# Expert 0's rows: seven tiles gathered ahead, the last added by one-hot products; W1[0] split during the output projection; the last one-hots on GpSimd

## What is computed

```python
x = x + concat([yc, ya]) @ w_out
xn = rms_norm(x, norm_ffn_w)                    # the rows that the experts read
g = argmax(xn @ w_group + b_group)              # 1 of 4 groups
top2 of (xn @ w_expert + b_expert)[group g]     # 2 of its 8 experts
h = silu(xb @ w1[e]) * (xb @ w3[e])             # for each of 32 experts, on its tokens xb
x = x + gate * (h @ w2[e])
```

## Time and profile before

| | us |
|---|---|
| median of three runs | 1163.4 (1162.27 to 1164.91) |
| the profiled execution, its own time | 1164.24 |
| its span in the trace | 1162.1 |
| PE busy | 1096.3 (94%) |
| DVE busy | 900.1 (77%) |
| ACT busy | 718.6 (62%) |
| mixer | 0 to about 419 |
| output projection and routing | about 419 to 550 |
| experts | about 550 to 1122 |
| scatter, read back, combine, store | 1122 to 1162 |

### The profile page before, as it was taken

The page is one execution under the profiler, slowest core; times in us unless marked ns, Lnnn a source line. Parts: engine busy times, 40 slices in busy tenths (PEclk is TensorE's granted clock), DMA queues, the critical chain, the costliest instruction groups (busy, mean ns, idle before and its releaser), DMA issues. The chain is left out here.

```text
span 1162.1 us, 16798 instructions
## 1 busy us (share of the span) xinstructions
PE 1096.3 (94%) x5766; PEld 894.9 (77%) x5766; DVE 900.1 (77%) x1033; ACT 718.6 (62%) x882; POOL 139.7 (12%) x192
## 2 busy tenths in 40 slices
PE   8999999999999899997999999999999999999950
PEld 7887777778777668885878888888888888888840
DVE  5505957678575772567989999999999999999947
ACT  5423555646643571112878888888888888888830
POOL 1001000010000120001021110111111111101000
PEclk9999999999999999997999999999999999999985
DMA  7111231313213253003999999999999999999529
GB/s 232 46 35 39 90 89 59 107 39 107 67 46 95 103 214 142 37 37 133 425 427 422 396 384 396 386 384 396 382 383 390 382 392 383 390 387 387 214 77 375
DMA packets 77117, 275.29 MB, mean 237 GB/s; under 512 B 20752, under 2 KB 51600, under 8 KB 63888
## 3 DMA queue, kind: packets, MB, share of 16 engines
q1 hardware_dynamic: 66272, 253.69, 57.6%
q0 software_dynamic: 9216, 16.80, 3.8%
q10 hardware_dynamic: 1584, 4.20, 0.9%
HBM read 259.57 MB, written 31.85 MB: 251 GB/s over the span
## 5 line engine op out<-in xcount | busy, mean ns | idle before, releaser
L1198 DVE TENSOR_TENSOR e_lo<-W,e_hi 128x1024 fp32r<-128x1024 f32 x384 | 451.9, 1219 | 24.5 <-ACT e_hi L1192 21.7
L1192 ACT ACTIVATE e_hi<-W 128x1024 fp32r<-128x1024 f32 x384 | 403.4, 1060 | 94.7 <-PE ps L1163 88.7
L1161 PE MATMUL ps<-e_hi,xT_hi 128*128 128x512 f32 x496 | 196.3, 396 | 1.9 <-DVE xT_lo L1920 1.0
L1163 PE MATMUL ps<-e_lo,xT_hi 128*128 128x512 f32 x496 | 193.7, 390 | 0.0
L1162 PE MATMUL ps<-e_hi,xT_lo 128*128 128x512 f32 x496 | 193.1, 389 | 0.0
L472 PE MATMUL ps<-xnT_hi,w_hi 128*128 128x512 f32 x320 | 129.0, 403 | 1.6 <-DVE u L861 0.6
L472 PE MATMUL ps<-xnT_hi,w_lo 128*128 128x512 f32 x320 | 128.0, 400 | 0.0
L472 PE MATMUL ps<-xnT_lo,w_hi 128*128 128x512 f32 x320 | 125.3, 392 | 0.0
L900 DVE TENSOR_TENSOR_SCAN kept<-kept,start_at 128x1024 f32<-128x1024 f32 (+7 forms) x64 | 88.9, 1389 | 29.1 <-ACT kept L702 29.1
L1161 PEld LDWEIGHTS ps<-e_hi,xT_hi 128*128 128x128 f32 x496 | 93.5, 189 | 20.9 <-DVE xT_lo L1920 1.2
L1163 PEld LDWEIGHTS ps<-e_lo,xT_hi 128*128 128x128 f32 x496 | 93.1, 188 | 19.9
(11 more groups left out here) (244 smaller groups left out, 1706.9 us busy)
## 6 DMA issues: line engine op xcount, KB each, us to landing
W<-in_w_dram SPq DMA_DIRECT2D x96, 2048.0 KB, 15.2
w_raw<-in_w_in_dram SPq DMA_DIRECT2D x20, 512.0 KB, 4.1
yy<-y_rows SPq DMA_DIRECT2D x7, 1024.0 KB, 12.7
xt<-in_x_dram SPq DMA_DIRECT2D x8, 512.0 KB, 3.7
w_out_raw<-in_w_out_dram SPq DMA_DIRECT2D x8, 512.0 KB, 6.4
xn_rows<-xn SPq DMA_DIRECT2D x8, 512.0 KB, 2.6
out_dram<-x ACTq DMA_DIRECT2D x7, 512.0 KB, 9.1
x<-in_x_dram SPq DMA_DIRECT2D x2, 1536.0 KB, 10.7
```

The costliest lines, as they stand in the source:

```text
L1161: pe.matmul(o, xs_hi[:, k], e_hi[:, p, cols], start=(k == 0), stop=False)
L1163: mm = pe.matmul(o, xs_hi[:, k], e_lo[:, p, cols], start=False, stop=(k == last))
L1192: act.activation(e_hi[:, p], flat[:, p * D:(p + 1) * D], ACT.Copy).then_inc(s["hi_made"], 1)
L1198: dve.tensor_tensor(e_lo[:, p], flat[:, p * D:(p + 1) * D], e_hi[:, p], ALU.subtract).then_inc(s["lo_made"], 1)
```

## The change

- DVE makes, in `rank`, a code of each token of expert 0 (its rank plus one, or zero), and from it one one-hot matrix for each tile (`first_one_hots`). PE's `first_list` multiplies seven of them by token numbers, DVE writes `first_token`, and GpSimd gathers expert 0's rows of tiles 0 to 6 while tile 7 is still being routed. `first_rows_gathered` multiplies them by the identity into the banks of `xT`, in accumulation; `first_rows_last` adds tile 7's rows, which are still in SBUF in `xn2[1]`, by its one-hot. `first_turn_x` goes.
- The order on PE: `first_rows_gathered` and two products of the table stand ahead of the count of tile 7; the table's last two products stand between the two halves of gate 0. The 34 transposes that nobody reads go.
- ACT and DVE split W1[0] in tiles 5 and 6 of the projection, into buffers of its own (`e0_hi`, `e0_lo`); W3[0] then needs no free piece.
- The last four pairs of one-hots are made by GpSimd, after the first gather. `xg[1]` is gathered when the whole table is made.
- PE in round 0: gate 0, two pieces of up 0, turn of the overflow list, two pieces of up 0, turn of `xg[1]`. DVE in round 0: pieces 0, 1 of W3[0], `pick_blocks`, piece 2, `list_blocks`, piece 3, gates, piece 0 of W1[1], `x1T_lo`, piece 1.
- SP: W3[0] and W1[1] when `xg[0]` has landed, W3[1] when `xg[1]` has landed, W2[0] after the list is turned, W1[2] after gate 0.

```diff
@@ SP
                 for m in range(NT):
-                    if m == NT - 1:
-                        sp.wait_ge(mixed, 2 * NT)
-                        sp.dma_start(W3[0], w3_v[0]).then_inc(expert_w[0][1], 16)
...
+                sp.wait_ge(mixed, 2 * NT)
                 sp.wait_ge(s_e["gathered"][0], 16)
+                sp.dma_start(W3[0], w3_v[0]).then_inc(expert_w[0][1], 16)
                 sp.dma_start(W1[1], w1_v[1]).then_inc(expert_w[1][0], 16)
+                sp.wait_ge(s_e["gathered"][1], 16)
                 sp.dma_start(W3[1], w3_v[1]).then_inc(expert_w[1][1], 16)
...
+                sp.wait_ge(s_e["freed"], used(gate_start(0) + PIECES))
                 load(W1, w1_v, 2, 0, 0, gate_start(0))
@@ GpSimd
-                for b in range(2):
-                    pool.wait_ge(xn2_stored[b], 16 * (NT // 2))
+                pool.wait_ge(xn2_stored[0], 16 * (NT // 2))
+                pool.wait_ge(xn2_stored[1], 16 * (NT // 2 - 1))
+                pool.wait_ge(first_listed, 1)
+                gather_rows(pool, xg[0], first_token, s_e["gathered"][0], S - P)
+                for n in range(HOTS - 4, HOTS):
+                    k, m = n % 2, n // 2
+                    pool.wait_ge(placed, 3 + m - (NT - 2))
+                    pool.wait_ge(table_step, n - NOH + 1)
+                    pool.tensor_scalar(of_slot[n % NOH], iota[:, 0:P], slot[:, k, m:m + 1], None, ALU.is_equal).then_inc(hot_late, 1)
+                    pool.tensor_scalar(of_column[n % NOH], iota_column, column[:, k, m:m + 1], pair_code[k][:, m:m + 1],
+                                       ALU.is_equal, ALU.mult).then_inc(hot_late, 1)
+                pool.wait_ge(xn2_stored[1], 16 * (NT // 2))
                 pool.wait_ge(routed, 1)
-                for e in range(2):
-                    gather_rows(pool, xg[e], slot_token[:, e:e + 1], s_e["gathered"][e])
+                gather_rows(pool, xg[1], slot_token[:, 1:2], s_e["gathered"][1])
@@ PE
                     if m == 7:
+                        count_before(2)
                         route(7, 0)
-                        count_before(2)
...
+                def first_list():
+                    bank, c0 = FIRST_AT
+                    pe.wait_ge(first_hots, NT - 1)
+                    for m in range(NT - 1):
+                        mm = pe.matmul(ps[:, bank, c0:c0 + 1], first_hot[:, m], token_less[:, m:m + 1], start=(m == 0), stop=(m == NT - 2))
+                    mm.then_inc(first_summed, 1)
+
+                def first_rows_gathered():
+                    pe.wait_ge(s_e["gathered"][0], 16)
+                    pe.wait_ge(x2_made, 2 * NT)
+                    for k in range(KT):
+                        pe.matmul(psf[:, k * P:(k + 1) * P], xg[0][:, k:D:KT], ident, start=(k % 4 == 0), stop=False)
+
+                def first_rows_last():
+                    pe.wait_ge(first_hots, NT)
+                    pe.wait_ge(xn2_made, NT + 1)
+                    for h in range(2):
+                        for k in range(4 * h, 4 * h + 4):
+                            mm = pe.matmul(psf[:, k * P:(k + 1) * P], xn2[1][:, k:D:KT], first_last, start=False, stop=(k % 4 == 3))
+                        mm.then_inc(s_e["turned"] if h else half_turned, 1)
...
+                first_list()
                 turn(NT - 1, 1)
                 route(NT - 1, 1)
+                first_rows_gathered()
+                table(12, 14)
                 count_before(3)
                 count_all()
-                table(12, 16)
-                for i in range(20):
-                    pe.transpose(ps[:, 4, 0:P], ident, ident)
...
+                first_rows_last()
...
                 def first_gate():
...
+                    pe_product(pe, s_e, 0, xT_hi, xT_lo, [ps[:, 2]], 2, KT - 1, (0, 1), **own)
+                    table(14, 16)
                     pe.wait_ge(s_e["xT_made"], 1)
...
+                        pe_product(pe, s_e, up_start(0), xT_hi, xT_lo, [ps[:, 3]], 2, KT - 1, (0, 1))
+                        overflow_list()
+                        pe_product(pe, s_e, up_start(0), xT_hi, xT_lo, [ps[:, 3]], 2, KT - 1, (2, 3))
+                        pe_turn_x(pe, s_e, 1, 1, 1)
+                        return
@@ ACT
+                        if m == 5:
...
+                            act_split(act, s_e, gate_start(0), W1[0], hi=e0_hi, free=True)
...
+                    act_split(act, s_e, up_start(e), W3[b], free=isinstance(e, int) and e == 0)
                     if isinstance(e, int) and e == 0:
+                        act.wait_ge(s_e["freed"], used(gate_start(0) + PIECES))
                         act_xT(act, s_e, 1)
@@ DVE
+                    link(dve.scalar_tensor_tensor(first_code[:, ms], earlier[:, :, 0], 1.0, chosen[:, ms, 0], ALU.add, ALU.mult))
+                    if i == 3:
+                        first_one_hots(NT - 1, NT)
...
+                        dve.wait_ge(first_summed, 1)
+                        dve.tensor_scalar(first_token, ps[:, FIRST_AT[0], FIRST_AT[1]:FIRST_AT[1] + 1], 4.0 * S, None, ALU.add).then_inc(first_listed, 1)
...
                     if isinstance(e, int) and e == 0:
-                        dve_split(dve, s_e, gate_start(0), W1[0], (2, 3))
+                        dve_split(dve, s_e, up_start(0), W3[0], (0, 1))
+                        pick_blocks()
+                        dve_split(dve, s_e, up_start(0), W3[0], (2,))
+                        list_blocks()
+                        dve_split(dve, s_e, up_start(0), W3[0], (3,))
                         make_gates()
...
+                        dve_split(dve, s_e, gate_start(1), W1[1], (0,))
                         dve_xT(dve, s_e, 1)
-                        dve_split(dve, s_e, gate_start(1), W1[1], (0, 1))
+                        dve_split(dve, s_e, gate_start(1), W1[1], (1,))
                         dve_hid(dve, s_e, 0, up_start(0))
...
+                ask_gates()
                 flag_blocks()
+                dve.wait_ge(table_step, HOTS)
+                slots(slice(0, NE))
```

More of the change, by code:

```diff
@@ L1151, in pe_turn_x, with pe_product @@
             mm.then_inc(s["turned"], 1)
-        def pe_product(pe, s, start, xs_hi, xs_lo, out, per_piece, last, pieces=range(PIECES)):
+        def pe_product(pe, s, start, xs_hi, xs_lo, out, per_piece, last, pieces=range(PIECES), hi=e_hi, lo=e_lo):
             for p in pieces:
@@ L1624, in round_of @@
                 def round_of(e, b, rounds, y_rounds=None, last=False):
[L1625 removed]
+                    if not (isinstance(e, int) and e <= 1):
                         act.wait_ge(expert_w[b][0], 16 * rounds)
```

140 lines of the change are left out of this document (81 added, 59 removed).

## The result

| | before | after |
|---|---|---|
| median, six runs each | 1163.53 us (1162.27 to 1165.78) | 1169.12 us (1168.17 to 1169.71) |
| the profiled execution, its own time | 1164.24 | 1169.59 |
| its span | 1162.1 | 1167.9 |
| last matmul of the output projection, start | 529.78 | 531.21 |
| gate 1, start | 563.26 | 567.58 |

The ratio of the medians is 1.0044, 95% interval 1.0031 to 1.0057: the changed kernel is 3.6 to 6.6 us slower. The forecast was 1164.1 with a range to 1167.8, so the prediction was wrong, on the slow side. By the trace the step that failed is the first: expert 0's rows let gate 0 start 3.6 us later than was added up.

A forecast was written before the change was run, and what follows sets the result against it. PE bounds the expert loop, and ACT's queue set gate 1. Gate 1 at -0.8 us, clock +2.5 and the W3[2] wait -1.0 sum to +0.7, so the median goes from 1163.4 to 1164.1 us, range 1160.4 to 1167.8.

The forecast's parts named there:

- Expert 0's rows: From the projection's end to gate 0: gate 0 starts at 543.8, 6.6 us earlier; bounds 542.3 to 545.2.
- W1[0] ahead: Projection tiles 5 and 6: the early split costs nothing or a few tenths, and takes 4.7 us of DVE out of round 0.
- GpSimd's one-hots: Between the halves of gate 0: four operations at most 3.6 us, ready at 546.4, so nothing is paid.
- the very price that was taken from above: One-hots before gate 0's second half: GpSimd's dearest small copy, 0.89 us, four are 3.6.
- Round 0: Gate 0 to gate 1: DVE ends up 0 at 556.4, then 6.1 us of chain; gate 1 at 562.5, 0.8 us earlier.
- the 1.1 us kept for it: W3[0] before up 0: by the nearest rows it lands at 547.7, 1.1 us too late; kept for the range.
- The clock: Gate 1: the clock falls in PE's idle 5 us before it, and half rate costs 2.5 us.
- The transfers: Weights from W3[1] to W3[2]: landed by 580.1, before ACT asks at 583.3; the 0.96 us wait at 588.15 goes.
- The second rival: Weights behind xg[1]: one lands 22 us after issue, not 11; gate 1 or up 1 waits 3 us: 1167.2; chance 0.16.
- The sum: Whole kernel: -0.8 at gate 1, +2.5 clock, -1.0 for W3[2], = +0.7 us; median 1164.1.
- The third rival: Before tile 7's count: late gather or GpSimd at twice its price makes PE wait; with 2 us 1166.2; chance 0.12.
- the three signs named for being wrong: Hole before gate 1 shorter than 4 us; tile 7's count starting before 539.5; DVE not holding up 0.

The follow-up runs named there:

- the lone split: The kernel before, with W1[0] split during tiles 5 and 6 of the projection and the buffers and SyncE wait that go with it: 1163.53 us, ratio 0.9996.
- the run that filled the hole: The changed kernel, with 34 transposes that nobody reads on PE behind the turn of xg[1]: 1167.23 us, ratio 1.003.
- the chain is cut: The changed kernel with xg[1]'s turn, list_blocks, silu and tile 7's count reordered: 1162.32 us with W3[1] issued early, 1167.67 with it behind xg[1].

## Why the prediction was wrong, by its own steps

Times after are those of the trace less 1.43, so that the projection ends at the same point.

| step | predicted | measured |
|---|---|---|
| first list | 1.5 us | 1.62 |
| the early rows land | 536.6 | 538.1 |
| `first_rows_gathered`, to the next product | 3.4 us | 3.8 |
| first half of `first_rows_last` | 1.0 us | 2.0 |
| gate 0 starts | 543.8 | 547.4 |
| one-hots of GpSimd ready | 546.4 or earlier | 548.6 |
| last piece of W3[0] ends on DVE | 555.0 | 558.5 |
| up 0 ends, turn of `xg[1]` starts | 556.4 | 560.1 |
| turn to gate 1 | 6.1 us | 6.07 |
| gate 1 starts | 562.5 | 566.15 |
| clock | +2.5 us | +2.19 |
| the wait for W3[2] | -1.0 us | -1.20 (-1.47 with the rest of the loop) |
| tail | nothing | +0.76 in the trace |

**Expert 0's rows: the term that failed.** Gate 0 was put at 543.8, with a bound of 545.2 for half clock throughout, and came at 547.4: 3.6 us late, and outside the bound. Two terms were mis-sized, the landing of the gather and the strided products. The gather landed 1.5 us late: 1.1 us passed on GpSimd between the token column and the launch (the profile calls it issue), where 0.1 was put, and before showed the same 1.1 ahead of its gather at 543.66; from launch to turn it took 5.16 and not 4.6. That 4.6 was one row: in the five traces of the kernel before and runs made from it, launch to turn is 4.5 to 5.6. The products were priced by transposes, which cost 0.125 us a record at full clock; with a strided stationary operand in true fp32 a record takes 0.25 at full clock. The run with neighbouring columns shows what that is worth: 0.4 us in the first block, whose 3.44 is then what was put, and 1.2 us from the second block to gate 0, where 2.63 then stands against 2.47. The landing and the stride together are 3.1 of the 3.6 us; the rest is in small steps, 0.3 of it in the two products of the table, the counts and DVE's answer. The bound was made from the same transposes at half clock, so it could not hold this: the row of another kind of instruction was taken as a bound of this one.

**W1[0] ahead** was right as far as it was tested: it costs nothing in the projection, and alone it gains nothing. The text's condition, that relief for DVE counts only if DVE bounds round 0, agrees with the lone split, where W1[1]'s landing and ACT let gate 1 go. In the changed kernel DVE does hold up 0; no run takes the split out there, so what it is worth in the change is not shown.

**GpSimd's one-hots** took 0.60 and 1.23 us, 3.6 for the four, the very price that was taken from above; VectorE's own in this trace take 0.28 and 0.41. The table's last products found them ready. The Trainium skill, GPSIMD Engine Reference, section Engine selection, puts GpSimd at about twice VectorE's time with two inputs and near its rate with one. These have one tensor input and a scalar or two for each partition, and took 2.1 and 3 times as long; the measurement decides.

**Round 0** was right in its mechanism and its lengths: DVE's low parts end it (the last piece waits 0.60 us for one), 12.7 us from gate 0 to the turn against 12.6, then the chain of 6.07 with ACT as the one that lets gate 1 go, then a clock of 0.5. It passed on the lateness of gate 0 without taking any back. W3[0] landed in time, so the 1.1 us kept for it were not needed.

**The clock** was right: 2.2 us, by the trace, and 2.2 by the trace of the run that filled the hole. It fell while PE was idle, and came back 4.7 us after work resumed.

**The transfers**: the wait for W3[2] went, worth 1.20 us rather than 0.96, since the turn ahead of it was not overlapped either. It also went in the run with the lone split and in the one with four waits more on SyncE, where gate 1 comes 0.6 us later, so it is no gain of the change's own. The second rival, late weights, was given 0.16 and did not happen. It was rightly seen as a limit, though one that decides only once the chain is cut, and then at up 2 rather than at gate 1 or up 1.

**The sum.** 3.7 us too little at gate 1, 0.3 too much for the clock, 0.5 too little gained behind it (0.2 at W3[2], 0.3 elsewhere in the loop), 0.8 forgotten in the tail, and 1.43 less 0.45 outside the stretch: 0.7 + 3.7 - 0.3 - 0.5 + 0.8 + 1.0 = 5.4, as the profiled executions differ (5.35). The third rival, with 0.12, had half of it: PE's wait in front of the count, each us there one at gate 1. The count started at 542.5, where the prediction's steps give 540.6, so about 1.9 of the 3.65 us at gate 1 lie in front of it, from the landing and the first block; the other half lies behind it and belongs to no rival. None of the three signs named for being wrong came: the hole before gate 1 was 5.02 us and ended by silu, the count started after 539.5, and DVE held up 0. The path was right, and the sizes on its first stretch were not. Whether the projection itself is a little slower after the change is open: its last matmul starts at 529.3 to 531.4 in five traces of the kernel before and runs made from it, and at 529.8 to 531.3 in nine of the changed kernel and runs made from it in which DVE writes `xn2` in order.

## What to carry to other kernels

Count what a reordering puts back into series before counting what it brings forward: here one turn moved behind a product laid 6 us of ACT's queue bare, and the idle time cost another 2 us of clock. A price can safely be borrowed only from the same kind of instruction with the same access pattern; where no such row exists, the bound has to say so and be wide. When a chain is cut, look for the transfer that comes next: the same cut was worth 6.5 us with one weight issued early and about 1 without, by the ratios.

## What the runs showed of the hardware

- A true fp32 product whose stationary operand is read with a stride of eight columns costs 0.25 us a record against 0.13 with neighbouring columns (weight load 335 against 191 ns), at full clock. A transpose with the same stride costs 0.13 us a record (load 188 ns); with neighbouring columns its load takes 139 ns, and 30 turns of eight together take 0.8 us less.
- VectorE writing 128x1024 fp32 with a stride of 128 columns takes 2.06 us, and 1.29 in order.
- From the last input of an indirect gather of 128 rows of 4 KB to its launch on GpSimd 1.1 us pass, and 5.16 more in the changed kernel until PE starts on the rows (4.5 to 5.6 in the five traces of the kernel before and runs made from it).
- 34 transposes kept the clock at 1.00 through a wait (560.9 to 564.8). 14 of them in a wait at 534.7 did not: it was at 0.50 from 535.3 on, with PE at work, and stayed there until 542.1. In three traces the clock was at 1.2 GHz for 3.4 us within gate 0 (from 546.4, 546.5 and 547.3), with PE at work before and during it.
